# Identity products in TensorE's waits, and other durations in a planner: a two-block model on one Trainium2 core

## The reference

```python
def first_block(x, ...):
    h = rmsnorm(x, mix_norm_g[l])
    proj = h @ w_in[l]                       # q, k, v of three attentions, and gates
    ...
    merged = gates[:, :, 0] * o_a + gates[:, :, 1] * o_d + gates[:, :, 2] * o_m
    x = x + merged @ w_out[l]
    h2 = rmsnorm(x, ffn_norm_g[l])
    u = causal_depthwise_conv(h2 @ w_ffn_up[l], ffn_conv_w[l], ffn_conv_b[l])
    u_gate, u_val = jnp.split(u, 2, axis=-1)
    x = x + (jax.nn.silu(u_gate) * u_val) @ w_ffn_down[l]

def second_block(x, ...):
    for l in range(2):
        h = rms_norm(x, norm1_g[l])
        proj = h @ w_in[l]
        ...
        mixed = jnp.concatenate([y_att, y_conv, y_rnn], axis=-1)
        x = x + mixed @ w_out[l]
        h2 = rms_norm(x, norm2_g[l])
        x = x + peer(h2, ...)
    return rms_norm(x, final_g)

def peer(xn, wq, k1, k2, u_tab, v_tab):
    ...                                       # keys, two top-16, 8 x 16 experts a token
    hid = jax.nn.gelu(jnp.einsum("td,tkd->tk", xi, u_tab[ei]))
    return jnp.einsum("tk,tkd->td", gi * hid, v_tab[ei])
```

## Time and profile before

| | us |
|---|---|
| median of 3 runs | 2053.2 (2052.7 to 2058.16) |
| profiled execution, its own time | 2048.43 |
| span of its trace | 2046.6 |
| busy: PE / DVE / ACT / POOL | 1666.4 / 1406.5 / 817.2 / 610.9 |
| DMA: moved, mean rate over the span | 770.09 MB, 376 GB/s |

### The profile page before, as it was taken

The page is one execution under the profiler, slowest core; times in us unless marked ns, Lnnn a source line. Parts: engine busy times, 40 slices in busy tenths (PEclk is TensorE's granted clock), DMA queues, the critical chain, the costliest instruction groups (busy, mean ns, idle before and its releaser), DMA issues.

```text
span 2046.6 us, 20781 instructions
## 1 busy us (share of the span) xinstructions
PE 1666.4 (81%) x6676; PEld 963.3 (47%) x6676; DVE 1406.5 (69%) x3607; ACT 817.2 (40%) x2072; POOL 610.9 (30%) x516
## 2 busy tenths in 40 slices
PE   8999989998889888886778877876887887756555
PEld 4449856583477464472326434532553463221111
DVE  4324327468776478866887876888887688877776
ACT  2423213433488236423444553333455324432222
POOL 0000000021422324523443343244425324454542
PEclk9999989899989999898889889988998899887878
DMA  9686868469999999999999999999999999999997
GB/s 391 211 312 237 298 227 279 170 222 388 386 419 419 420 418 407 420 418 407 420 420 419 419 419 420 399 420 420 419 420 412 416 354 419 419 420 420 421 420 306
DMA packets 108382, 770.09 MB, mean 376 GB/s; under 512 B 12144, under 2 KB 12656, under 8 KB 16368
## 3 DMA queue, kind: packets, MB, share of 16 engines
q0 software_dynamic: 73728, 536.90, 63.7%
q1 hardware_dynamic: 34544, 231.85, 29.4%
HBM read 767.65 MB, written 1.05 MB: 376 GB/s over the span
## 4 chain that ended last, share of the span: by engine, by line
PE 39%; DMA 37%; DVE 10%; issue 8%; ACT 3%; POOL 3%; SPq 0%; DVEq 0%; POOLq 0%
DMA arena<-in_peer_dram,eidx 10%; DMA ring<-in_peer_dram,eidx 10%; PE psum L1109 9%; DMA ring<-in_slabs_dram 9%; PE psum L745 8%; PE psum L768 8%; PE psum L954 6%; DMA kv<-in_peer_dram,eidx 5%; DMA early<-in_peer_dram,eidx 3%; PE psum L971 3%; DVE x L2023 2%; DVE arena L2013 1%; POOL arena L2165 1%; POOL ring L2165 1%; PE psum L786 1%
## 5 line engine op out<-in xcount | busy, mean ns | idle before, releaser
L2165 POOL DMA_INDIRECT arena<-in_peer_dram,eidx x203 | 244.8, 1206 | 832.5 <-DVE eidx L1885 440.2
L1109 PE MATMUL psum<-arena,diag 128*128 128x512 f32 x548 | 307.5, 694 | 109.1 <-ACT diag L1441 108.6
L1431 ACT ACTIVATE wexp<-wexp 128x1 f32<-128x1 f32 x512 | 103.2, 202 | 676.2 <-DVE wexp L2013 674.5
L2013 DVE CUSTOM_DVE_ANT_0 arena<-arena,osb 128x1024 f32<-128x1024 f32 x203 | 247.0, 1221 | 79.6 <-DMA arena<-in_peer_dram,eidx 76.8
L1109 PE MATMUL psum<-ring,diag 128*128 128x512 f32 x428 | 225.8, 661 | 61.4 <-ACT diag L1441 60.8
L2165 POOL DMA_INDIRECT ring<-in_peer_dram,eidx x155 | 185.0, 1193 | 295.8 <-PE psum L1109 234.3
L745 PE MATMUL psum<-ring,hT 128*128 128x512 f32 x560 | 258.6, 613 | 16.7 <-DMA ring<-in_slabs_dram 14.6
L1109 PEld LDWEIGHTS psum<-arena,diag 128*128 128x128 f32 x548 | 111.7, 216 | 269.6 <-ACT diag L1441 160.2
L2013 DVE CUSTOM_DVE_ANT_0 ring<-ring,osb 128x1024 f32<-128x1024 f32 x155 | 188.4, 1221 | 58.9 <-DMA ring<-in_peer_dram,eidx 57.0
L1109 PE MATMUL psum<-kv,diag 128*128 128x512 f32 x284 | 158.8, 688 | 53.3 <-ACT diag L1441 52.9
L954 PE MATMUL psum<-hT,ring 128*128 128x130 f32 x1408 | 168.0, 282 | 12.6 <-DMA ring<-in_slabs_dram 11.8
(11 more groups left out here) (328 smaller groups left out, 2131.0 us busy)
## 6 DMA issues: line engine op xcount, KB each, us to landing
ring<-in_slabs_dram SPq DMA_DIRECT2D x200, 1024.0 KB, 4.9
ring<-in_slabs_dram SPq DMA_DIRECT2D x8, 768.0 KB, 4.1
kept<-in_slabs_dram SPq DMA_DIRECT2D x4, 1024.0 KB
arena<-in_peer_dram,eidx POOLq DMA_INDIRECT x203
ring<-in_peer_dram,eidx POOLq DMA_INDIRECT x155
ring<-in_slabs_dram SPq DMA_DIRECT2D x4, 512.0 KB
kk<-in_keys_dram SPq DMA_DIRECT2D x2, 1024.0 KB, 8.9
kv<-in_peer_dram,eidx POOLq DMA_INDIRECT x105
```

The lines of the kernel that those rows point to most:

```text
L1109: ins = pe.matmul(bank(b), diags_of(n), pair(slot_of[n])[:, 1024 + 512 * h:1536 + 512 * h], start=(k == 0), stop=(k == 127))
L1431: act.activation(wn, wn, ACT.Gelu_apprx_tanh).then_inc(*up("gelu", n))
L2013: v.tensor_tensor_reduce(out=row, in0=row, in1=row_y[t], scale=1.0, scalar=0.0, op0=ALU.mult, op1=ALU.add, accum_out=wexp[:, c:c + 1]).the ...
L2165: pool.indirect_dma_start(pair(i), None, tables, bass.IndirectOffsetOnAxis(ap=eidx[:, 128 * t + k:128 * t + k + 1], axis=0)).then_inc(sig. ...
```

## The change

1. A new helper, turns(b, n, tile), issues n products of 128 columns of the identity with itself (at the very start: of a block of zeros) into a PSUM bank that nothing uses at that point. The run-through doesn't see them. They stand ahead of or behind eight waits of TensorE in B0 and M00: START (8 ahead of the first turn, 9 behind it), MERGE (5, 2), NORM (18, 2), LAST (5 behind the last ffn product), MIX (16 and 2 around M00's first turn, 3 ahead of the wait for the attention output, 2 ahead of the waits for its copy, 4 ahead of the turn of the second norm). 76 in all.
2. POOL writes zeros to the first diagonal block at its start, for START.
3. The run-through's durations are other numbers: T_DOT 1.35 to 1.16, T_WEIGHT 0.55 to 0.52, T_TENSOR 2.1 to 1.8, T_VECTOR 1.35 to 1.21; a product of 128 columns 0.232 to 0.225 and the fixed part of wider ones 0.02 to 0.01; the fixed part of a vector instruction 0.2 to 0.12, and of one with a reduction 0.28 to 0.2.

```diff
+START, MERGE, NORM, LAST, MIX = (8, 9), (5, 2), (18, 2), 5, (16, 2, 3, 2, 4)
...
-T_MB, T_SEEN, T_ISSUE, T_DOT, T_WEIGHT, T_DIAG, T_TENSOR, T_VECTOR, ... = 2.5, 2.0, 1.15, 1.35, 0.55, 0.42, 2.1, 1.35, ...
+T_MB, T_SEEN, T_ISSUE, T_DOT, T_WEIGHT, T_DIAG, T_TENSOR, T_VECTOR, ... = 2.5, 2.0, 1.15, 1.16, 0.52, 0.42, 1.8, 1.21, ...
...
     def matmul(self, out, lhsT, rhs, **k):
-        return self.run(max(0.232, 0.02 + 0.00166 * wide(rhs)) * (0.75 if lhsT.shape[0] <= 64 else 1.0))
+        return self.run(max(0.225, 0.01 + 0.00166 * wide(rhs)) * (0.75 if lhsT.shape[0] <= 64 else 1.0))
...
     def _vector(self, out, src, *a, **k):
-        return self.run(0.2 + 0.00107 * max(wide(out), wide(src)))
+        return self.run(0.12 + 0.00107 * max(wide(out), wide(src)))
...
     def tensor_tensor_reduce(self, out, in0, **k):
-        return self.run(0.28 + 0.00107 * wide(in0))
+        return self.run(0.2 + 0.00107 * wide(in0))
...
-            def turn_tile(s, src, banks, turned, after, *key):
+            def turns(b, n, tile=ident):
+
+                if measured or not n:
+                    return
+                wait_bank(b)
+                for _ in range(n):
+                    pe.matmul(bank(b)[:, 0:128], tile, tile, start=True, stop=True)
+
+            def turn_tile(s, src, banks, turned, after, *key, spare=None, idle=0):
 
                 for h in range(2):
                     b = banks[h]
+                    if h == 0:
+                        turns(spare, idle)
                     w.wait_ge(*after)
                     wait_bank(b)
...
+                if t == 0:
+                    w.wait_ge(sig.sem("blank"), 1)
+                    turns(b_[5], START[0], diag[:, 0:128])
                 w.wait_ge(sig.sem("l_id"), 16)
                 yield from turn_tile(s, x3[:, t, :], b_[6:8], "turned_v", (sig.sem("l_x%d" % t), 16), "h")
+                turns(b_[5], 0 if t else START[1])
                 w.wait_ge(*at("turned_v", s, "h", 1))
...
-                yield from turn_tile(s, scr_[:, 1024:2048], b_[6:8], "turned_v", at("scaled", s, "f"), "f")
+                yield from turn_tile(s, scr_[:, 1024:2048], b_[6:8], "turned_v", at("scaled", s, "f"), "f", spare=b_[5], idle=0 if t else NORM[0])
+                turns(b_[5], 0 if t else NORM[1])
                 w.wait_ge(*at("turned_v", s, "f", 1))
...
+                        if f == 21 and t == 0:
+                            turns(b_[5], LAST)
...
+                turns(b_[1], MIX[2] if s == "M00" else 0)
                 b = b_[0]
                 w.wait_ge(*at("att_out", s, 0))
...
         def gather_program(pool):
             w = Waits(pool)
             held = {}
+            pool.memset(diag[:, 0:128], 0.0).then_inc(sig.sem("blank"), 1)
```

More of the change, by code:

```diff
@@ L1043, in mixer @@
                 yield
+                turns(b_[1], MIX[3] if s == "M00" else 0)
                 w.wait_ge(*at("o_out", s))
```

11 lines of the change are left out of this document (7 added, 4 removed).

## The result

The changed kernel takes **2060.8 us** (median of 8 runs, 2058.1 to 2064.0) where the kernel before takes 2055.0 beside it: a ratio of 1.0033, 95% interval 1.0019 to 1.0047. It is slower by some 6 us, where 13 us less was forecast. The profiled execution has a span of 2059.9 us.

A forecast was written before the change was run, and what follows sets the result against it. TensorE was taken to bound the first 446 us, DMA the rest. 12.0 (clock) + 1.5 (start) + 0 (durations) = 13.5 us off 2048.4 gives 2034.9; with the runs' median 4.8 higher, 2040 us, range 2026 to 2062.

The forecast's parts named there:

- What bounds the kernel: TensorE until about 446 us, then full DMA: time TensorE wins before the first gather moves the end by the same amount.
- Do the products fit, and do they hold the clock: TensorE's waits in the first part: products fit the holes and keep the clock full, winning 12.0 us (0 to 12.9).
- The start: First 13.5 us: 8 and 9 products around the first turn raise the clock early, +1.5 us (-1.6 to +2.1).
- What is late next: Check in the first part: FFN slab loads keep up (2.5 us against 3.6); VectorE and ScalarE chains move with TensorE.
- The durations: New run-through numbers reorder steps, mainly affecting the DMA-bound stretch: taken as 0, bounds -15 and +25 us.
- The rival "slower": DMA-bound stretch: pairs queue behind other work on TensorE, three more holes lose 25 us, 2065 us; chance 0.14.
- clock not held: First part: the products do not hold the clock, nothing of the 12 us comes, 2056 us; chance 0.12.
- both parts pay: Clock held and nearer durations close half of the 26 us of DMA holes, 2027 us; chance 0.14.

The follow-up runs named there:

- e1: The kernel before plus the 76 products and POOL's zeros, all run-through durations as before; 2041.3 us.
- e5: As e1, but the fixed part of a vector instruction 0.177 us (0.257 with a reduction) instead of 0.2 (0.28); 2031.1 us.
- e8: As e1, but the fixed part of a vector instruction 0.26 us (0.34 with a reduction) instead of 0.2 (0.28); 2090.4 us.
- e2: The kernel before with the change's new run-through durations alone, no products; 2069.6 us.
- e3: As e1, but with the pairs' four numbers new (T_DOT 1.16, T_WEIGHT 0.52, T_TENSOR 1.8, T_VECTOR 1.21); 2038.6 us.
- e12: As e5, but with T_DOT 1.30 and T_TENSOR 2.24; 2038.6 us.

## Why the prediction was wrong, point by point

**What bounds the kernel: right.** Time is the first gather plus the bytes behind it plus the holes: first gather and holes add up to 470.3 us before, 480.5 after, 458.2 in e1, 447.8 in e5, 510.5 in e8, and what is left of the median (2055.0, 2060.8, 2041.3, 2031.1, 2090.4) is 1580 to 1585 us in all five.

**Do the products fit, and do they hold the clock: right.** The time lines of e1, TensorE's turns and its product for the attention output, and the first gather:

```profile
45.13 1.04 PE L797 MATMUL psum<-const,osb 128*128 128x128 f32 x8
...
132.44 1.28 PE L786 MATMUL psum<-const 128*128 128x128 f32 x10
134.11 1.09 PE L797 MATMUL psum<-const,scr 128*128 128x128 f32 x8 [0.40 <-DVE scr L1774]
...
154.98 1.09 PE L797 MATMUL psum<-const,scr 128*128 128x128 f32 x8 [1.02 <-DVE scr L1783]
...
275.24 1.09 PE L797 MATMUL psum<-const,x 128*128 128x128 f32 x8 [0.27 <-DVE x L1642]
...
280.54 1.09 PE L797 MATMUL psum<-const,arena 128*128 128x128 f32 x8 [0.63 <-DVE arena L1941]
...
364.17 0.66 PE L1061 MATMUL psum<-const,arena 128*128 128x128 f32 x4
...
365.52 8.85 PE L746 MATMUL psum<-ring,arena 128*128 128x512 f32 x20 [0.24 <-ACT arena L1381]
...
384.84 1.09 PE L797 MATMUL psum<-const,osb 128*128 128x128 f32 x8
...
428.69 1.08 POOL L2189 DMA_INDIRECT arena<-in_peer_dram,eidx  x1 [427.75 <-DVE eidx L1908]
```

The holes of the earlier trace rows are down to 0.40, 1.02, 0.27 and 0.63 us, at the end of M00's attention to none and 0.24, and before its second norm's turn to none. The granted clock, 0.50 in the earlier trace rows, stays at full through all of it; windows of e1 around the four places:

```profile
134.00:142.00 8.00, 7.59 (x26) 4.12 (x27) 0.06 (x1) 1.09 (x2) 0.00 (x0) 1.00 1.01 418
150.00:165.00 15.00, 13.48 (x119) 13.11 (x118) 5.46 (x17) 5.54 (x10) 0.00 (x0) 1.00 0.46 161
276.00:296.00 20.00, 18.47 (x150) 16.89 (x148) 9.60 (x37) 4.65 (x9) 0.00 (x0) 1.00 0.46 156
363.00:372.00 9.00, 8.63 (x32) 4.72 (x32) 8.01 (x20) 1.72 (x3) 0.00 (x0) 1.00 0.45 160
```

The same rows against the earlier trace rows size the terms one by one. Between turns e1 wins 1.55 us (134 to 155 us; forecast 1.6), 2.50 (155 to 275; 2.85), 2.87 (280 to 364; 3.7), 2.95 (364 to 385; 3.05) and 1.39 (385 to the first gather; 0.85): 11.3 us where 12.0 was forecast. The Trainium skill's page "TensorE: Matmul & The Clock Gate", Part 4, says that a transpose does not count as work for the clock as a matmul does; the products of the identity in plain form did count, as these windows show, where the turns alone had left it at 0.50 in the earlier trace rows.

**The start: right in sign, over-sized.** Forecast +1.5, measured 0.84. The trace of before has the next turn here:

```profile
45.81 1.04 PE L786 MATMUL psum<-const,osb 128*128 128x128 f32 x8
```

From the first token product that is 36.48 us before (9.33) and 35.64 in e1 (9.49 to 45.13). In e1 the windows at 10 and at 14 us hold 6 records of token products each, where the earlier trace rows has 3 and 6, so the products bring what the prediction said; but TensorE then reaches the end of its first slab before the second has landed, and gives 0.96 us back:

```profile
9.49 13.97 PE L746 MATMUL psum<-ring,hT 128*128 128x512 f32 x32 [0.66 <-DMA ring<-in_slabs_dram]
24.42 20.87 PE L746 MATMUL psum<-ring,hT 128*128 128x512 f32 x48 [0.96 <-DMA ring<-in_slabs_dram]
```

"What is late next" was asked for the FFN and not here. In the profiled execution of the kernel after, the first slab came at 10.69 us, the hole after the nine products was 2.51 us, and the clock fell back (0.86 at 10 to 12 us, 0.79 at 14 to 16): there the term is 0.37 us (36.11 us to the turn at 46.80).

**The durations: the step that failed.** They were taken at 0, "the value nearest to a stretch that runs at 98% of its rate", with bounds of -15 and +25. They cost 16.9 us (e2), inside the bounds, and more than the products win. Two arguments behind the 0 did not hold. First, "I see no row that gives a sign": the run-through's number was held against the busy column, but what a step takes on an engine is the distance from start to start, and rows of that kind stood in the trace of before. Here is a quarter of routing in it, from its first search to the dot behind it:

```profile
1282.82 0.50 DVE L1808 MAX8 sm<-psum 128x8 f32<-128x128 f32 x2 [6.59 <-PE psum L1075]
...
1294.88 1.22 DVE L2013 CUSTOM_DVE_ANT_0 arena<-arena,osb 128x1024 f32<-128x1024 f32 x1
```

It is 45 instructions of the kernel in 12.06 us. By the run-through's formula and their widths we estimate that it counts them as 10.0 us with 0.12, 12.6 with 0.177 and 13.6 with 0.20. So the change went from 1.5 us too long to 2.1 too short, past the value that fits. That was a reason against taking the new number as nearer, though not a price: only the runs show that 0.12, with the other new numbers, costs 17 to 19 us while 0.20 costs at most some 10 (e1 against e5). The two readings by which the prediction doubted the new numbers, 1.22 us for a dot and 2.24 for a pair, were of the busy column too and do not hold (last section). Second, that the stretch runs at 98% was taken as safety, while it says how well the old order happens to fit: the orders of 0.06, 0.22 and 0.26, and of 0.12 together with other new numbers, all have more holes.

**The rival "slower": right in sign and near in size (2065 forecast, 2060.8 measured), wrong in mechanism as a whole.** Holes did open, three large ones, but TensorE is not filled to the brim in them: it is 9.71 us busy of 20 at 1180 us, and it waits 9.26 us for diag at 1525 us. In the largest hole it is busy 101.20 of 120 us, but e5 has 103.72 there and no hole. At one place, the 26 us at 731.6, a pair did queue as the rival says; over the whole stretch from 440 to 2000 us the pairs did not queue longer, since from the end of diag to the pair's start on TensorE they wait 734 us in all after, 825 before and 751 in e5. e3 shows that 60 more pairs on TensorE cost nothing. The argument against this rival, that the choice between the engines shifts by a sixth of a microsecond only, was wrong in itself (101 pairs on VectorE after, 162 before) and of no weight.

**The rivals "clock not held" and "both parts pay"** did not occur.

## What to carry to other kernels

Fill TensorE's short waits with products of a constant where its clock falls: here 76 of them were worth 11 us, and each term could be read beforehand from the half-clock windows. Give a planner the start-to-start distance of an instruction as the trace shows it in the place that matters, not its busy time, and be as wary of a number that is too short as of one too long: here new durations, one of them some 0.05 us an instruction too short for routing, ate the whole gain, and mending that one gave it back. Then try a few neighbours, as equally good numbers gave orders from 2031 to 2042 us; the best of them, products with 0.177, beats the kernel before by 1.0% (ratio 0.9883 to 0.9913) and the changed one by 1.4%.

## What was not expected of the hardware

VectorE's busy column is neither the spacing of dependent instructions nor that of independent ones. Rows of VectorE in the kernel after: a chain in which each waits for the one before, six taps of the convolution of which each needs the one before last, dots one behind another; and two pairs on TensorE:

```profile
1507.04 0.18 DVE L1876 CAST junk<-smi 128x32 f32<-128x32 uint32 x1
1507.25 0.18 DVE L1878 TENSOR_SCALAR smi<-smi 128x32 uint32<-128x32 uint32 x1
1507.47 0.18 DVE L1880 CAST junk<-smi 128x32 f32<-128x32 uint32 x1
...
758.15 1.66 DVE L2116 SCALAR_TENSOR_TENSOR mixs<-keep,vecs,mixs 128x128 f32<-128x128 f32 x6
...
1533.29 1.22 DVE L2036 CUSTOM_DVE_ANT_0 kv<-kv,osb 128x1024 f32<-128x1024 f32 x1
1534.44 1.22 DVE L2036 CUSTOM_DVE_ANT_0 ring<-ring,osb 128x1024 f32<-128x1024 f32 x1
...
1541.02 1.88 PE L1132 MATMUL psum<-ring,diag 128*128 128x512 f32 x4
1542.73 1.88 PE L1132 MATMUL psum<-early,diag 128*128 128x512 f32 x4
```

The chain goes on every 0.215 us with 0.18 us busy; the formula with 0.12 gives 0.154, with 0.177 0.211, with 0.20 0.234. The taps go on every 0.28 us or less with 0.345 us busy each: there 0.12 (0.257) is nearer than 0.20 (0.337). The dots start 1.15 us apart, the reading of the sum included, with 1.22 and 0.08 us busy. So the change's T_DOT of 1.16 was right, the prediction's objection to it was not, and e12's 1.30 was no better number. The pairs on TensorE start 1.71 us apart here at full clock (granted 1.00 from 1541 to 1546 us), so the change's 1.8 was near as well, and the 2.24 of the prediction and of e12 was not. One fixed part cannot be right for the chain and for the taps.

The Trainium skill's page "VectorE: DVE Perf Modes", section "The DRAIN you can't avoid", says that the next instruction does not start before the pipeline has emptied, that one which is not held starts earlier, and that a semaphore between two instructions costs nothing extra. The first two fit these rows (0.035 us after the end in the chain, 0.07 us before it in the taps). The third, which the page gives for eight copies in a row, no run here tests: the chain and the taps differ in more than the wait.

The first slab does not land at the same time in every execution: at 9.49 us in e1's and at 10.69 in that of the kernel after. The nine products behind the first turn were followed by 0.66 us of waiting in e1, and the granted clock stayed at full; by 2.51 us in the kernel after, and it fell.
